# Queries of both attentions projected with tokens on partitions and turned by DMA transposes; weight blocks loaded in four pieces

## What is computed

```python
h = rms_norm(x, g_mix)
rq, rk, rv, rg, dq, dk, dv, mq, gates = split(h @ w_in)
# retention (4 heads, q/k width 256, v width 512), chunks of 128 tokens
# differential attention: 8 heads, two maps of width 64 each, causal
dqn = rms_norm(dq.reshape(B, S, 8, 2, 64), g_diff_q)
dkn = rms_norm(dk.reshape(B, S, 8, 2, 64), g_diff_k)
dif = diff_attention(dqn, dkn, dv, lam)          # softmax(map 0) - lam * softmax(map 1)
# cross-attention into 256 memory tokens: 4 heads of width 256
mk, mv = split(rms_norm(mem, g_mem) @ w_mem_kv)
mo = memory_attention(rms_norm(mq, g_mem_q), rms_norm(mk, g_mem_k), mv)
y = sigmoid(gate0) * (ret @ w_br_ret) + sigmoid(gate1) * (dif @ w_br_diff) + sigmoid(gate2) * (mo @ w_br_mem)
x = x + y @ w_o
```

## Time and profile before

| | |
|---|---|
| median of 3 runs | 2390.73 us (2389.24 to 2524.57) |
| profiled execution: own time | 2388.88 us |
| its span on the slowest core | 2387.8 us |
| spans of the 8 cores | 2382.2 to 2387.8 us |
| granted TensorE clock, mean | 0.995 to 0.997 of full |
| PE busy | 2321.8 us, 97% of the span |
| DVE, ACT, POOL busy | 1222.9, 984.8, 149.8 us |

### The profile page before, as it was taken

One profiled execution on the slowest core, in us unless ns is written; L12 is line 12 of the kernel. 1 busy time (PEld: TensorE's weight loads), 2 busy tenths in 40 slices (PEclk: granted clock), 3 DMA queues, 4 the chain that ended last, 5 costly groups with the idle time before them and its releaser, 6 DMA issues.

```text
span 2387.8 us, 34149 instructions; the slowest of 8 cores (2382.2 to 2387.8 us)
## 1 busy us (share of the span) xinstructions
PE 2321.8 (97%) x13284; PEld 1112.4 (47%) x13284; DVE 1222.9 (51%) x2359; ACT 984.8 (41%) x1679; POOL 149.8 (6%) x173
## 2 busy tenths in 40 slices
PE   6999999999999999999999999999999999999998
PEld 2444444444444444454444465555554444444443
DVE  5577334485565552113444576677754655344334
ACT  3111110357767764144631487788851221111110
POOL 1000000230000000000000111121100000000000
PEclk9999999999999999999999999999999999999999
DMA  8221221353442424342102200201305322321313
GB/s 232 49 50 24 52 38 34 82 135 58 67 79 37 83 43 74 54 73 51 20 16 46 46 12 10 45 13 28 48 10 141 71 45 36 53 36 24 47 18 141
DMA packets 86779, 132.69 MB, mean 56 GB/s; under 512 B 71648, under 2 KB 72032, under 8 KB 75360
## 3 DMA queue, kind: packets, MB, share of 16 engines
q0 software_dynamic: 10512, 75.50, 18.8%
q1 hardware_dynamic: 76112, 55.00, 9.1%
HBM read 172.43 MB, written 16.78 MB: 79 GB/s over the span
## 4 chain that ended last, share of the span: by engine, by line
PE 90%; ACT 4%; DVE 2%; POOL 1%; DMA 1%; issue 1%; SPq 0%; POOLq 0%; DVEq 0%; ACTq 0%
PE pw L605 90%; ACT ET L616 2%; POOL acc L628 1%; ACT nrs L616 1%; DMA stg<-w_ffn_in 1%; DMA memT<-mem 0%; ACT L616 0%; DVE dq L620 0%; DVE dU L639 0%; ACT sqf L616 0%; SPq L647 0%; DVE mqn L620 0%; DVE dn L620 0%; ACT nsq L616 0%; ACT sgt L616 0%
## 5 line engine op out<-in xcount | busy, mean ns | idle before, releaser
L605 PE MATMUL pw<-hT,wbuf 128*128 128x512 bf16 x4864 | 1168.5, 381 | 12.3 <-ACT nrs L616 5.6
L605 PEld LDWEIGHTS pw<-hT,wbuf 128*128 128x128 bf16 x4864 | 471.5, 98 | 551.9 <-issue 29.4
L616 ACT ACTIVATE sgf<-pw 128x512 f32<-128x512 f32 x176 | 104.1, 596 | 702.6 <-PE pw L605 702.5
L605 PE MATMUL pw<-uu,wbuf 128*128 128x512 bf16 x1408 | 334.1, 379 | 0.0
L605 PE MATMUL pw<-wbuf,hT 128*128 128x512 bf16 x1280 | 303.2, 379 | 0.2 <-DVE sgR L628 0.2
L616 ACT ACTIVATE ET<-pw 128x1024 bf16<-128x1024 f32 (+1 forms) x288 | 265.9, 975 | 66.9 <-PE pw L605 64.0
L628 DVE TENSOR_TENSOR uu<-pw,sgf 128x512 bf16<-128x512 f32 x176 | 120.8, 690 | 275.7 <-PE pw L605 275.5
L605 PEld LDWEIGHTS pw<-uu,wbuf 128*128 128x128 bf16 x1408 | 137.7, 98 | 166.1 <-issue 0.2
L605 PEld LDWEIGHTS pw<-wbuf,hT 128*128 128x128 bf16 x1280 | 123.0, 98 | 137.5 <-issue 0.6
L605 PE MATMUL pw<-Vd,ET 128*128 128x129 bf16 x2176 | 173.2, 220 | 8.3 <-DVE dU L639 4.5
L620 DVE SCALAR_TENSOR_TENSOR xT<-pw,xT 128x512 f32<-128x512 f32 x192 | 130.4, 688 | 78.4 <-PE pw L605 74.7
(11 more groups left out here) (120 smaller groups left out, 2153.6 us busy)
## 6 DMA issues: line engine op xcount, KB each, us to landing
wbuf<-w_in POOLq DMA_DIRECT2D x26, 1024.0 KB, 8.3
wbuf<-w_ffn_in POOLq DMA_DIRECT2D x21, 1024.0 KB, 10.3
wbuf<-w_ffn_out POOLq DMA_DIRECT2D x10, 1024.0 KB, 9.6
xs<-xT SPq DMA_DIRECT2D x4, 2048.0 KB, 11.6
xT<-x SPq DMA_DIRECT2D x6, 1024.0 KB, 22.9
wbuf<-w_br_ret POOLq DMA_DIRECT2D x4, 1024.0 KB, 8.0
wbuf<-w_mem_kv POOLq DMA_DIRECT2D x4, 1024.0 KB, 10.5
x2l<-xs SPq DMA_DIRECT2D x2, 2048.0 KB, 14.5
```

Source lines behind the costliest of these rows:

```text
L605: return Op("pe", lambda e: e.matmul(out, lhsT=lhsT, rhs=rhs, start=start, stop=stop, **kw), reads, writes, n / 2400.0 + 0.003, 0.17, sign ...
L616: return Op("act", lambda e: e.activation(out=out, in_=in_, func=func, **kw), reads, writes, c, 0.08, fuse=("accum_out" not in kw), tab=TA ...
```

## The change

1. **Memory attention.** `m_proj` makes the query projection with `hT` as the stationary operand: 128 tokens on partitions, 512 query columns (two heads) per bank. New `m_q`: ACT squares each half with a running sum (`accum_out`), Ln and Exp work on 128 x 2, DVE scales, and a DMA transpose turns the 128 x 512 tile into `mqn`. `m_core` no longer sums denominators on PE: the values `mvT` get a column of ones, the second product has 257 columns and tokens on partitions, DVE takes a reciprocal and scales, and a DMA transpose writes `MO`. These are 32 + 32 transposes.
2. **Differential attention.** The columns of `w_in` are repacked so that one block holds queries and keys of two heads. A step of `d_proj` covers 256 tokens: 16 matmuls of 256 columns in place of 8 of 512. New `d_qk`: ACT squares, DVE multiplies by the gains into `qraw` and sums by groups of 64, Ln and Exp on 128 x 8, POOL scales, and a DMA transpose writes `dqk`. These are 64 transposes; the 64 matmuls with `bd64` are gone.
3. **Weights.** `pump` is gone. A stream `loader` issues each block as four DMAs of 1024 columns. A piece is handed over when the scheduler's PE clock has moved 4.5 us since the piece before (`GAP`), or at once when a stream already asks for this block (`want`). Each piece is made to wait for the last PE instruction with a semaphore that has been written so far (`op.toks`). Streams wait (in the order, not on the chip) until all four pieces are written before they write the block's first matmul.
4. **Smaller ones.** The scheduler supposes the memory tokens 8 us later than before (`memTb.w_fin`), the merge after retention starts under a weaker condition, `d_tail` uses the shared `nsq` buffers (4 in place of 3) and `dn` is gone, and pacing numbers in `d_proj` change (3 pairs in place of 4).

```diff
+PIECE = 1024
+GAP = 4.5
+LAND = 3.0
...
-    def pump(self):
-        while self.avail and self.issued < len(self.plan):
-            self.P.emit(self.load())
+    def loader(self):
+        P = self.P
+        last = [P.t["pe"]]
+        while self.issued < len(self.plan):
+            yield lambda: bool(self.avail)
+            tag = self.plan[self.issued]
...
+            for i in range(n // PIECE):
+                yield lambda: P.t["pe"] >= last[0] + GAP or self.want == tag
+                last[0] = P.t["pe"]
...
+                op.chain = k
+                if P.count[P.eid["pe"]]:
+                    op.toks = [(P.eid["pe"], P.count[P.eid["pe"]])]
+                yield op
...
+            self.full.add(tag)
 
     def there(self, tag):
-        k = self.where.get(tag)
-        return k is not None and (self.bufs[k].claimed or tag == self.plan[0])
+        if tag in self.full or tag == self.plan[0]:
+            return True
+        self.want = tag
+        return False
...
+                    yield lambda: W.there(("rg", h))
                     wgt, wgb = W.take(("rg", h))
...
+        def m_q(b, mi, c, key):
...
+            for hh in range(2):
+                s1 = mss[:, u * 2 + hh:u * 2 + hh + 1]
...
+                yield act(nrs[j][:, 0:256], bk(b)[:, hh * 256:hh * 256 + 256], AF.Square, [bkb[b]], [nrsb[j], mssb[u]], 256,
+                          accum_out=s1)
...
+            yield flip(mqn[mi][:, c * TT:(c + 1) * TT].rearrange("p (a q) -> p a q", a=4), nsq[n][:, :], [nsqb[n]],
+                       [mqnb[mi][c]], 131072)
...
-            for mt in range(2):
-                yield mm(bk(b), ones1, EM[es_[mt]][:, :], mt == 0, mt == 1, [EMb[es_[mt]], b_cbf], [bkb[b]], TT)
...
+                        yield mm(bk(b)[:, 0:257], EM[e][:, c * 128:(c + 1) * 128], mv4[:, mt, hm, 0:257], mt == 0, mt == 1,
+                                 [mvTb, EMb[e]], [bkb[b]], 257)
...
+        def d_qk(b, h, i):
...
+            yield act(nrs[j][:, :], bk(b), AF.Square, [bkb[b]], [nrsb[j]], TT)
...
-            yield mm(bk(m), bd64, nsq[i][:, :], True, True, [nsqb[i], b_cbf], [bkb[m]], TT)
...
+            yield flip(sl.rearrange("p (a n) -> p a n", a=4), nsq[n][:, :], [nsqb[n]], [dqkb[h % 2][i]], 131072)
...
-                    for k in range(KC):
-                        o = k * 512 + hl * 128
-                        yield mm(bk(b), wt[:, o:o + 128], hs(t, k), k == 0, k == KC - 1, [wb, hTb[t][k]], [bkb[b]], TT)
-                    sch.spawn(d_qk(b, which, h, t), 2)
+                    for cc in range(2):
+                        for k in range(KC):
+                            o = k * 512 + (h % 2) * 256
+                            yield mm(bk(b)[:, cc * 256:cc * 256 + 256], hcol(i // 2, k, (i % 2) * 2 + cc), wt[:, o:o + 256],
+                                     k == 0 and cc == 0, k == KC - 1 and cc == 1, [wb, hTb[i // 2][k]], [bkb[b]], 256,
+                                     group=False)
+                    sch.spawn(d_qk(b, h, i), 2)
```

More of the change, by code:

```diff
@@ L59 @@
 class Op:
-    __slots__ = ("eng", "fn", "reads", "writes", "cost", "lat", "sig", "fuse", "tab", "dma", "rows", "soon", "held")
+    __slots__ = ("eng", "fn", "reads", "writes", "cost", "lat", "sig", "fuse", "tab", "dma", "rows", "soon", "held",
+                 "chain", "toks")
     def __init__(self, eng, fn, reads, writes, cost, lat=0.0, signal=True, fuse=True, tab=None, dma=None, rows=128):
@@ L83, in __init__ @@
             self.dma_sem_ids[q] = ids
+        self.dma_rr = {"sp": 0, "pool": 0}
+        self.chain_sids = []
+        for i in range(4):
+            self.chain_sids.append(len(self.sems))
+            self.sems.append(es.enter_context(nc.semaphore(f"d_w{i}")))
         self.nclk = len(self.sems)
@@ L464, in build_program @@
         ssq = fixed("ssq", 8, F32)
+        qss = fixed("qss", 32, F32)
+        mss = qss
+        gqk = fixed("gqk_sb", 256, F32)
         dss = fixed("dss", 16, F32)
         drc = fixed("drc", 32, F32)
-        nsq = [fixed(f"nsq{i}", TT, BF16) for i in range(3)]
+        nsq = [fixed(f"nsq{i}", TT, BF16) for i in range(4)]
         nrs = [fixed(f"nrs{i}", TT, F32) for i in range(2)]
@@ L1258, in m_core @@
+        def m_core(t, hm, mi, key):
+            for c in range(4):
+                yield flag((key, c))
+            q4 = mqn[mi][:, :].rearrange("p (c a q) -> p c a q", c=4, a=4)
             es_ = []
             for mt in range(2):
+                yield EM_s.free
+                e = EM_s.get()
+                es_.append(e)
                 yield mk_pool.free
@@ L1333, in d_qk @@
-            d_main.put(m)
-            yield act(nrs[j][:, :], nrs[j][:, :], AF.Exp, [nrsb[j]], [nrsb[j]], TT, scale=-0.5)
-            dst, db, g = (dq[pp], dqb[pp], PV_GDQ) if which == 0 else (dk[pp], dkb[pp], PV_GDK)
-            yield stt(dst[:, t * TT:(t + 1) * TT], qraw[r][:, :], pvec[:, g:g + 1], nrs[j][:, :], ALU.mult, ALU.mult,
-                      [qrawb[r], nrsb[j], b_const], [db[t]], TT)
-            nrs_s.put(j)
-            qraw_s.put(r)
-            flags.add(("dqk", h, t, which))
+            yield qss_s.free
@@ new lines, in d_qk @@
+            u = qss_s.get()
+            ss = qss[:, u * 8:u * 8 + 8]
+            yield Op("dve", lambda e: e.reduce_sum(out=ss, in_=nrs[j][:, :].rearrange("p (g d) -> p g d", g=8),
+                                                   axis=mybir.AxisListType.X), [nrsb[j]], [qssb[u]], 0.7)
+            nrs_s.put(j)
+            yield act(ss, ss, AF.Ln, [qssb[u], b_eps], [qssb[u]], 60, bias=epsc[:, 0:1], scale=1.0 / 64.0)
+            yield act(ss, ss, AF.Exp, [qssb[u]], [qssb[u]], 60, scale=-0.5)
@@ L1342, in d_vev @@
+            nsq_s.put(n)
+            flags.add(("dqk", h, i))
         def d_vev(b, g, c):
@@ L1570, in main @@
             g_banks = pool_of(0, 1, 2)
[L1571 removed]
+            yield lambda: len(Tm_s.held) == 0
             sch.spawn(m_first(), 4)
```

279 lines of the change are left out of this document (162 added, 117 removed).

## The result

The changed kernel takes 1.0058 times as long as before (95% interval 1.0034 to 1.0082); it took 2403.6 and 2404.3 us, against a median of 2390.6 us for before. 2385 us were forecast, so the sign was wrong. Three of its five executions, and some of most other kernels' (before's too), ran slower with a lower clock on four or on all eight cores; no time in this document comes from them.

The account below looks back on a forecast made before the run. PE was taken to bound the kernel (busy 2321.8 of 2387.8 us). Terms -27.6 + 1.8 - 4.9 + 21.9 + 1 + 2 + 8 - 8 = -5.8 gave 2385 us for the median; 8-in-10 range 2361 to 2411 us.

Parts of the forecast that it names:

- weight pieces at the head boundaries: Retention's three head boundaries (edges): PE waits 5.6 us for rg's last two pieces, plus 1.7 of clock, each; +21.9 us.
- the pieces are not felt at the heads: Rival for retention's head boundaries: the 21.9 us of loss there do not come, 2363 us; chance 0.14.
- Start of retention: POOL's squares for the norm have DMAs in between, each now waiting for PE: +2 us (0 to 6).
- Memory tokens and other blocks: PE's idle time and lost clock at memT go, -4.9 us; last pieces of blocks outside rg barely covered, +1 us.
- Memory attention: Waits for transposes and scaling, with SP, ACT and DVE all near PE's 83 us: +8 us (0 to 26).
- the rival that put 26 us there: Memory attention: transposes bound it, 3.3 us of PE wait at each of 8 blocks, 2403 us; chance 0.18.
- Differential attention: Waits for nrs and dq go, ACT has 20 us less work: -8 us (-18 to +4), besides the matmuls taken away.
- that rival: Differential attention was held by ACT: all 20 us of PE's idle time come back, 2373 us; chance 0.10.
- the matmuls cut finer: Value product 13.8 to 14.0 us and projection 110.6 to 112.0 us, in narrower matmuls: together +1.8 us.

Follow-up runs that it names:

- attn_alone: The changed kernel with the weight loading of before (whole blocks, issued when a buffer is given back): 2433.6 and 2437.4 us.
- attn_oldcost_ret: attn_alone with the old supposition on transposes (landing after all DMAs issued before) up to the memory attention: 0.9971, 2384 us.
- pieces_oldcost_ret: The changed kernel, paced pieces everywhere, with the old supposition on transposes in retention alone: 1.0063, 2406 us.
- mixed_late: The changed kernel with whole blocks up to the last m_kv block, paced pieces behind, and the old supposition on transposes up to retention's end: 0.9919, 2372 us.
- ret_at_once: The changed kernel with pacing and the wait for PE's progress taken from retention's blocks rqk, rv and rg alone: 1.0043, 2400 us.
- gap25: The changed kernel with 2.5 us of PE's work between two pieces (GAP) in place of 4.5: 1.0018, 2395 us.

## Why the prediction was wrong

**The failed step: weight pieces at the head boundaries.** The place, the number and the kind of wait are as forecast: three waits for `wbuf`, one head apart, with the clock at half behind. Its size was not: +28.2 us against +21.9. On the slowest core the waits were 7.9, 6.7 and 6.8 us in place of 5.6. The sum let the load begin when PE stops. In the trace the first of the two pieces is issued 0.5 us after that and the last one 1.1 us after it, which I had put at nothing. From its own issue the last piece then took 6.6, 5.5 and 5.7 us: at two boundaries what I had for two pieces (5.55), at the first 1.1 us more. Two transposes of `kT` were on their way each time, but no run here singles out why the first one is longer. The 10.6 us of the earlier trace rows are no better guide: they are the median of two loads, of which the needed one took 8.1 us, as if alone, and the one behind it 13.2. The clock cost 2.7 us at the first boundary, 1.9 at the second and 1.4 at the third, so the 1.7 that I gave was about right. With a boundary at 9.4 us instead of 7.3, the term is 6.3 us short.

**The step that was missing: the supposition on transposes.** I took the new cost for a part of the attentions, but the planner uses it in retention too. With whole blocks it alone costs 40 us at the edges (attn_alone against attn_oldcost_ret). In the changed kernel it happens to cost little (3.1 us), since the order that the pieces bring stops PE at the same three places (pieces_oldcost_ret). My rival "the pieces are not felt at the heads" was therefore wrong in a way that I could not see: take the pacing away and the other cause appears (2400 to 2409 us, not 2363); with both gone it is still 2390.

**Start of retention.** +2 forecast, +2.4 measured, in part by luck: with whole blocks (attn_alone) the same part is 1.9 us shorter than before, so the pieces cost 4.3 us there, and something else, which no run singles out, gave 1.9 back. **Rest of retention.** No term; +2.7 measured, of which 1.3 us is the wait for merge mr's first block, whose 5.0 us of cover I had thought enough.

**Memory tokens and other blocks.** -4.9 and +1 forecast, -0.4 measured. The wait behind `memT` went, and pieces of `m_kv`'s blocks took its place: 5.8 us on the slowest core. I had set 5.6 and 6.1 us of PE's work against a landing of 5.6, the same lone-load figure, and given the result almost nothing. mixed_late shows that these waits go with whole blocks.

**Memory attention.** Its waits came to 11.4 us in place of 3.0, so +8.4 against +8; they are for the transposes of `mqn` and for DVE's scaling, as forecast, and the rival that put 26 us there falls. That its 2403 us is what was measured is luck: the time came from retention. The stage gained 2.9 us and not 5.6; its clock is 0.99 where it was 1.00, some 2 us of the rest.

**Differential attention.** -20.3 forecast, -17.4 measured. The matmuls count in full; PE's waits fell from 19.5 to 14.7 us, by 5 and not by 8. 4.7 of what is left is one new wait, for DVE's `qraw` before the first scores. ACT's work in the stretch fell from 344 to 328 us; all of the recorded idle time did not come back, so that rival falls too. The stretch of 425 us took 409, against some 405 forecast.

All terms erred on one side, by 6.3 us (edges), 3.5 (tokens and blocks), 2.7 (memory attention), 2.9 (differential attention), 2.7 (rest of retention) and 0.4 (its start). Their sum, 18.5 us, is the miss: -5.8 to +12.7. The range held the time, being wide. The direction hung on the edges: their 6.3 us alone turn -5.8 into +0.5. (14.0 - 13.8 and 112.0 - 110.6 add to 1.6 us and not to the 1.8 that I wrote for the matmuls cut finer, which changes nothing. And PE's busy time fell by 16 us and not by some 25, because half speed stretches it by 18.5 us, against 6.7 before.)

## What to carry to other kernels

Where a scheduler writes the order, a changed cost acts on every stage that has such an operation; compare the lists of the stages that you believe untouched before you predict. Two causes that stop an engine at the same place hide each other in part, and taking either away alone shows too little (pieces_oldcost_ret 3 us of the edges' 28 and ret_at_once 9, both together 17): change both. Spread the loads where short DMAs are on the path, and issue them whole and at once where a block has only some 13 us from its buffer coming free to its first matmul.

## What was unexpected of the hardware

In the traces of before and after no transpose on SP's queue landed ahead of a weight load that POOL's queue had issued before it. A transpose landed in 2.4 us alone, in 7.8 us beside pieces some 2 us apart (gap25), and in 17.0 us when it was issued between two whole loads (attn_alone), behind the second too, which was issued 1.0 us after it. Pieces queued closely land mostly 1.3 to 1.6 us apart, so a block in four pieces flows about as fast as a whole one; as a whole it lands some 2 us later (10.2 against 8.1 us). Two short stops of PE cost almost as much again by the clock: 2.9 and 1.6 us of waits brought 3.4 us of half speed (pieces_oldcost_ret). PE's busy time is no measure of its work where the clock falls: 11.8 us lie between two kernels with equal matmuls.
